# Second norm of three bridges from cross sums gathered in the layer ahead, residual update and scaling in one stream

## The reference

```python
def rms_norm(x, g):
    y = x * lax.rsqrt(jnp.mean(x * x, axis=-1, keepdims=True) + RMS_EPS)
    return y * g

x = x + gate * rms_norm(y, g1)                 # first norm and residual update
h = rms_norm(x, g2) * (1 + scale) + shift      # second norm, on the updated residual
out = squared_relu_mlp(h, w1, w2)              # or the next layer's projections
```

## Time and profile before

| | |
|---|---|
| median of 3 runs | 3150.22 us |
| profiled execution, time | 3138.47 us |
| profiled execution, span | 3136.6 us |
| mean granted TensorE clock | 0.953 of 2.4 GHz |
| TensorE matmul busy | 2850.1 us (91%) |
| VectorE busy | 1775.9 us (57%) |
| ScalarE busy | 1215.9 us (39%) |
| bridge A, first `grow` to the end of the first pair of products | 377.3 to 427.8 us |
| bridge B, the same | 1968.7 to 2004.0 us |
| bridge C, the same | 2349.6 to 2383.9 us |

### The profile page before, as it was taken

One profiled execution on the slowest core, in us unless ns is written; L12 is line 12 of the kernel. 1 busy time (PEld: TensorE's weight loads), 2 busy tenths in 40 slices (PEclk: granted clock), 3 DMA queues, 4 the chain that ended last, 5 costly groups with the idle time before them and its releaser, 6 DMA issues. The chain is left out here.

```text
span 3136.6 us, 66277 instructions
## 1 busy us (share of the span) xinstructions
PE 2850.1 (91%) x29060; PEld 2480.2 (79%) x29060; DVE 1775.9 (57%) x2747; ACT 1215.9 (39%) x1998; POOL 35.7 (1%) x57
## 2 busy tenths in 40 slices
PE   4988999999997997899989988899999898889998
PEld 4977989999996887677777776788877685778877
DVE  7655565645446644666666644655546644466632
ACT  4225343222224433555555543433324425354421
POOL 0011000000002000000000000000000000000000
PEclk9999889999996998999999998799998999999999
DMA  6320223343321323000000103255531210123322
GB/s 254 121 86 28 81 84 128 124 141 125 124 79 58 108 95 127 31 25 16 18 25 26 32 7 115 109 179 182 175 111 53 64 41 8 54 81 99 97 86 82
DMA packets 89980, 272.89 MB, mean 87 GB/s; under 512 B 9440, under 2 KB 14688, under 8 KB 89568
## 3 DMA queue, kind: packets, MB, share of 16 engines
q1 hardware_dynamic: 85088, 258.17, 24.3%
q10 hardware_dynamic: 4608, 10.49, 0.9%
HBM read 252.11 MB, written 16.52 MB: 86 GB/s over the span
## 5 line engine op out<-in xcount | busy, mean ns | idle before, releaser
L430 DVE TENSOR_TENSOR weights_low<-raw_weights,weights_high 128x1024 fp32r<-128x1024 f32 (+3 forms) x333 | 356.5, 1072 | 741.5 <-ACT weights_high L399 740.9
L399 ACT ACTIVATE weights_high<-raw_weights 128x1024 fp32r<-128x1024 f32 (+3 forms) x333 | 310.8, 935 | 993.7 <-PE psum L223 954.0
L223 PE MATMUL psum<-mlp_in_high,weights_high 128*128 128x512 f32 (+1 forms) x1120 | 371.2, 368 | 17.8 <-DVE mlp_in_low L861 12.8
L223 PE MATMUL psum<-mlp_in_low,weights_high 128*128 128x512 f32 (+1 forms) x1120 | 370.2, 367 | 0.0
L223 PE MATMUL psum<-mlp_in_high,weights_low 128*128 128x512 f32 (+1 forms) x1120 | 369.9, 367 | 0.0
L223 PEld LDWEIGHTS psum<-mlp_in_high,weights_high 128*128 128x128 f32 x1120 | 208.6, 190 | 45.0 <-issue 13.9
L223 PE MATMUL psum<-hidden_low,weights_high 128*128 128x384 f32 (+1 forms) x768 | 229.8, 353 | 0.0
L223 PE MATMUL psum<-hidden_high,weights_high 128*128 128x384 f32 (+1 forms) x768 | 229.7, 353 | 0.0
L223 PE MATMUL psum<-hidden_high,weights_low 128*128 128x384 f32 (+1 forms) x768 | 229.7, 353 | 0.0
L223 PEld LDWEIGHTS psum<-mlp_in_high,weights_low 128*128 128x128 f32 x1120 | 208.7, 190 | 24.3
L223 PEld LDWEIGHTS psum<-mlp_in_low,weights_high 128*128 128x128 f32 x1120 | 208.8, 190 | 24.0
(11 more groups left out here) (451 smaller groups left out, 5599.0 us busy)
## 6 DMA issues: line engine op xcount, KB each, us to landing
mod_space<-in_ada SPq DMA_DIRECT2D x112, 512.0 KB, 3.9
raw_weights<-in_mlp_w SPq DMA_DIRECT2D x96, 512.0 KB, 4.3
raw_weights<-in_w_up SPq DMA_DIRECT2D x44, 512.0 KB, 3.6
work<-in_ada SPq DMA_DIRECT2D x32, 512.0 KB, 5.1
raw_weights<-in_mlp_w SPq DMA_DIRECT2D x64, 256.0 KB, 3.0
raw_weights<-in_w_down SPq DMA_DIRECT2D x16, 512.0 KB, 3.5
raw_weights<-in_w_in SPq DMA_DIRECT2D x12, 512.0 KB, 4.8
raw_weights<-in_w_out SPq DMA_DIRECT2D x8, 512.0 KB, 3.9
```

The source lines that it names most:

```text
L223: last = nc.tensor.matmul(out[:, a, :] if wide else out, w[:, cols], x[:, at, t0:t1], start=first, stop=final)
L399: nc.scalar.activation(halves_of(ph, j)[0], raw_of(ph, j), ACT.Copy).then_inc(high.sem, 1)
L430: nc.vector.tensor_tensor(lo, raw_of(ph, j), hi.bitcast(F32), ALU.subtract).then_inc(split.sem, 1)
```

## The change

`CrossSums` takes the place of `FoldedSums` at the end of the three blocks ahead of the bridges. Beside the running total of y*y it keeps two more: of X*u and of u*u. Per tile ScalarE squares twice (the second time with the gain as its scale), and VectorE makes the product X*u and folds three totals (two of u*u and X*u and the old one). The gains `0x mix` and `0c mix` are derived one block earlier, and the buffers are reused (`pool_u` stays alive as the space of `Sides`).

`MergedBridge` takes the place of `Bridge`. TensorE sums the two cross totals (`cross`) behind the first spread; four small VectorE operations (`update`) correct the kept sum of squares of X; the second root comes from that. The residual need not be squared. The update of the later tiles and the scaling of the first ones run in one VectorE stream, five tiles apart. `grow` works in place in y, which also takes the scaled tile. Two earlier roots (opening of layer 0, token shift of layer 1) copy their sums of squares into `residual_squares` (one ScalarE copy each).

```diff
+class CrossSums:
...
+    def square(self, eng, k):
+        act = self.core.nc.scalar.activation
+        if k >= 2:
+            eng.wait_ge(self.folded.sem, self.step(k - 1, "y"))
+        act(self.sq if k else self.total, self.y(k), ACT.Square).then_inc(self.squared.sem, 1)
+        if k >= 2:
+            eng.wait_ge(self.folded.sem, self.step(k - 1, "gy"))
+        for t0, t1, c in self.gains:
+            last = act((self.gy if k else self.total_gy)[:, t0:t1], self.y(k)[:, t0:t1], ACT.Square, scale=col(c, k))
+        last.then_inc(self.squared.sem, 1)
+
+    def fold(self, dve, k):
+        nc = self.core.nc
+        dve.wait_ge(self.squared.sem, self.squared0 + 2 * k + 1)
+        if k >= 2:
+            dve.wait_ge(self.folded.sem, self.step(k - 1, "xy"))
+        for t0, t1, c in self.gains:
+            last = nc.vector.scalar_tensor_tensor((self.xy if k else self.total_xy)[:, t0:t1], self.y(k)[:, t0:t1], col(c, k),
+                                                  self.x(k)[:, t0:t1], ALU.mult, ALU.mult)
+        last.then_inc(self.folded.sem, 1)
+        if k == 0:
+            return
+        if k < self.kt - 1:
+            nc.vector.tensor_tensor(self.total, self.total, self.sq, ALU.add).then_inc(self.folded.sem, 1)
+        dve.wait_ge(self.folded.sem, self.step(k, "product"))
+        nc.vector.tensor_tensor(self.total_xy, self.total_xy, self.xy, ALU.add).then_inc(self.folded.sem, 1)
+        dve.wait_ge(self.squared.sem, self.squared0 + 2 * k + 2)
+        nc.vector.tensor_tensor(self.total_gy, self.total_gy, self.gy, ALU.add).then_inc(self.folded.sem, 1)
...
+    def cross(self, pe):
+        pe.wait_ge(self.folded.sem, self.step(self.kt - 1, "gy"))
+        for place, total in ((self.place_xy, self.total_xy), (self.place_gy, self.total_gy)):
+            for t in range(self.tokens // P):
+                last = self.core.nc.tensor.matmul(place[:, t:t + 1], total[:, t * P:(t + 1) * P], self.core.ones[:, 0:1],
+                                                  start=True, stop=True)
+        last.then_inc(self.crossed.sem, 1)
+
+    def update(self, dve, first):
+
+        nc, nt = self.core.nc, self.tokens // P
+        r, t, kept = first.small[:, 1, :], first.small[:, 3, :], self.core.residual_squares[:, 0:nt]
+        chain = Chain(dve, self.steps, self.steps0)
+        dve.wait_ge(self.crossed.sem, self.crossed0 + 1)
+        chain(nc.vector.tensor_tensor(t, self.place_gy, r, ALU.mult))
+        chain(nc.vector.scalar_tensor_tensor(t, self.place_xy, 2.0, t, ALU.mult, ALU.add))
+        chain(nc.vector.tensor_tensor(t, t, r, ALU.mult))
+        chain(nc.vector.tensor_tensor(kept, kept, t, ALU.add))
...
 class Root:
...
-        eng.wait_ge(*sums.complete())
-        nc.scalar.activation(self.small[:, 0, :], sums.place[:, 0:self.nt], ACT.Sqrt, bias=self.core.eps,
+        if self.updated is None:
+            eng.wait_ge(*sums.complete())
+        else:
+            eng.wait_ge(*self.updated)
+        src = sums.place[:, 0:self.nt] if self.updated is None else self.core.residual_squares[:, 0:self.nt]
+        if self.keep:
+            nc.scalar.activation(self.core.residual_squares[:, 0:self.keep], src[:, 0:self.keep], ACT.Copy)
+        nc.scalar.activation(self.small[:, 0, :], src, ACT.Sqrt, bias=self.core.eps,
...
+class MergedBridge(Bridge):
...
+    def scalar(self, eng, weights):
+        self.first.scalar(eng)
+        weights()
+        self.root.scalar(eng)
+        for k in range(self.kt):
+            self.scaling.shift(eng, k)
+
+    def tensor(self, pe):
+        self.first.tensor(pe)
+        self.sums.cross(pe)
+        self.root.tensor(pe)
+
+    def vector(self, dve, weights):
...
+        self.first.vector(dve)
+        dve.wait_ge(*self.first.ready())
+        grow(0)
+        grow(1)
+        add(0)
+        weights()
+        grow(2)
+        add(1)
+        self.sums.update(dve, self.first)
+        grow(3)
+        add(2)
+        self.root.vector(dve)
+        grow(4)
+        add(3)
+        dve.wait_ge(*self.root.ready())
+        for k in range(self.kt + 1):
+            n = k + self.AHEAD
+            if n < self.kt:
+                grow(n)
+            if k < self.kt:
+                scale(k)
+            if n <= self.kt:
+                add(n - 1)
+            if k >= 1:
+                self.scaling.low(dve, k - 1)
```

More of the change, by code:

```diff
@@ L797, in add, with __init__, step, complete @@
         ins.then_inc(self.summed.sem, 1)
+class CrossSums:
+    def __init__(self, core, y, x, gains, kt, tokens, space, totals):
+        self.core, self.y, self.x, self.gains, self.kt, self.tokens = core, y, x, gains, kt, tokens
+        self.total, self.sq, self.xy, self.gy = (space[:, i * tokens:(i + 1) * tokens] for i in range(4))
+        self.total_xy, self.total_gy = (totals[:, i * tokens:(i + 1) * tokens] for i in range(2))
+        nt = tokens // P
+        self.place = core.psum[:, 7, 256:256 + nt]
+        self.place_xy, self.place_gy = (core.psum[:, 5, 256 + 8 * i:256 + 8 * i + nt] for i in range(2))
+        names = ("cross_squared", "cross_folded", "cross_summed", "cross_done", "cross_step")
+        self.squared, self.folded, self.summed, self.crossed, self.steps = (counter(core, n) for n in names)
+        self.squared0, self.folded0, self.summed0, self.crossed0, self.steps0 = \
+            (counter(core, n).base for n in names)
+        self.squared.base += 2 * kt
+        self.folded.base += 1 + 4 * (kt - 2) + 3
+        self.summed.base += 2
+        self.crossed.base += 1
+        self.steps.base += 4
+    def step(self, k, which):
+        if k == 0:
+            return self.folded0 + 1
+        order = ("product", "y", "xy", "gy") if k < self.kt - 1 else ("product", "xy", "gy")
+        return self.folded0 + 1 + 4 * (k - 1) + order.index(which) + 1
+    def square(self, eng, k):
[17 more added lines that the diff above has]
+        last.then_inc(self.folded.sem, 1)
+        if k == 0:
+            return
[5 more added lines that the diff above has]
+        nc.vector.tensor_tensor(self.total_gy, self.total_gy, self.gy, ALU.add).then_inc(self.folded.sem, 1)
+    def complete(self):
+        return self.summed.sem, self.summed0 + 2
+    def add(self, pe, k):
+        if k < self.kt - 2:
+            return
+        last, nt = k == self.kt - 1, self.tokens // P
+        if last:
+            pe.wait_ge(self.squared.sem, self.squared0 + 2 * k + 1)
+        else:
+            pe.wait_ge(self.folded.sem, self.step(k, "y"))
+        for t in range(nt):
+            ins = self.core.nc.tensor.matmul(self.place[:, t:t + 1], (self.sq if last else self.total)[:, t * P:(t + 1) * P],
+                                             self.core.ones[:, 0:1], start=not last and t == 0, stop=last and t == nt - 1)
+        ins.then_inc(self.summed.sem, 1)
+    def cross(self, pe):
[14 more added lines that the diff above has]
+        chain(nc.vector.tensor_tensor(kept, kept, t, ALU.add))
+    def updated(self):
+        return self.steps.sem, self.steps0 + 4
@@ L957, in vector, with grow, add, scale @@
         self.scaling.low(dve, self.kt - 1)
+class MergedBridge(Bridge):
+    AHEAD = 5
+    def scalar(self, eng, weights):
[9 more added lines that the diff above has]
+    def vector(self, dve, weights):
+        nc = self.core.nc
+        def grow(k):
+            for t0, t1, c in self.gains:
+                last = nc.vector.scalar_tensor_tensor(self.y[:, k, t0:t1], self.y[:, k, t0:t1], col(c, k),
+                                                      self.first.rstd[:, t0:t1], ALU.mult, ALU.mult)
+            last.then_inc(self.grown.sem, 1)
+        def add(k):
+            dve.wait_ge(self.grown.sem, self.grown0 + k + 1)
+            nc.vector.tensor_tensor(self.X[:, k, 0:self.tokens], self.X[:, k, 0:self.tokens], self.y[:, k, 0:self.tokens], ALU.add)\
+                .then_inc(self.added.sem, 1)
+        def scale(k):
+            dve.wait_ge(self.added.sem, self.added0 + k + 1)
+            self.scaling.scale(dve, k)
+        self.first.vector(dve)
[23 more added lines that the diff above has]
+                self.scaling.low(dve, k - 1)
 class Opening(Bridge):
@@ L3022, in folded_sums, with cross_sums, merged_bridge @@
             return FoldedSums(core, src, DT, tokens, space, core.psum[:, bank, 256:256 + tokens // P])
+        def cross_sums(tokens, gains, space, totals):
+            return CrossSums(core, lambda k: Y[:, k, 0:tokens], lambda k: X[:, k, 0:tokens], gains, DT, tokens, space, totals)
+        def merged_bridge(tokens, scales, shifts, dst, space, cross, y, gains):
+            first = Root(core, cross, wide(tokens, 6))
+            root = Root(core, cross, wide(tokens, 4), updated=cross.updated())
+            scaling = Scaling(core, DT, tokens, lambda k: X[:, k, 0:tokens], root.rstd, scales, shifts, dst, space)
+            scaling.tmp = [y[:, k, 0:tokens] for k in range(DT)]
+            return MergedBridge(core, tokens, X, root, scaling, cross, y, gains, first)
```

(5 more changed lines are left out.)

42 lines of the change are left out of this document (25 added, 17 removed).

## The result

| | before | after |
|---|---|---|
| median of the runs | 3149.73 us (3144.36 to 3152.85, 4 runs) | 3114.31 us (3110.60 to 3120.51, 4 runs) |
| ratio | | 0.9891, 95% interval 0.9868 to 0.9914 |
| profiled execution | 3138.47 us | 3111.34 us (span 3109.2) |

A forecast was written before the change was run, and what follows sets the result against it. TensorE, 91% busy, was taken as the bound, with time to win in its bridge waits: 9.8 (A) + 6.8 (B) + 6.3 (C) - 0.2 = 22.7 us, from 3150.2 to 3127.5 us, range 3119.5 to 3138.5.

The forecast's parts named there:

- the bridges: Hand-overs A (after layer 0's `w_out`), B (after `rw_wo`), C (after layer 1's MLP): gains of 9.8, 6.8 and 6.3 us.
- The entries: Block ends ahead of the bridges: product and folds behind the last square delay A 1.65, B 1.0, C 1.15 us.
- The stream: VectorE from first `grow` to `low` of tile 0: 13.5 us in B (before 21.2), 18.7 in A.
- The small chain is hidden: In the bridges: cross sums end before `update`; second root and spreading lie under 2.5 us of `grow` and `add`.
- The cover in `w_out`: Block ahead of A: VectorE's added 2.95 us per step fit into 3.69 us idle, 0.7 to spare.
- The kept copy: Token shift's root: ScalarE copy of the kept sums on the path, 0.1 to 0.25 us, counted as 0.2 lost.
- rival 1: Product pairs: low clock lasts twice as long, 3134 us, chance 0.10; or through the pair, 3150, chance 0.03.
- the term for what the clock gives back: Pair in B: ends at 1997.1 if the clock returns after 5.7 us, 1996.1 if at once.
- Rivals 2, 3 and 4: 2: VectorE bounds `w_out`, 3155 us, 0.04; 3: bridge's end off the path, 3150, 0.05; 4: stream holes, 3132, within forecast.
- the median of the runs lies 11.75 above, and I carry the difference over: Whole kernel: median 11.75 us above the profiled 3138.47, so base 3150.2 less 22.7 gives 3127.5.
- medians here differ by some 2 us: Whole kernel: room for median spread, used with gains of 12 to 29 us to set the range.

The follow-up runs named there:

- in_turn: Changed kernel with its cross sums, but VectorE back in the old order; 3132.51 us, ratio 0.9964 to the kernel before.
- load: Changed kernel plus two useless VectorE products in every `w_out` step ahead of bridges A and B; 3131.37 us, one run.
- before_again: The kernel before, unchanged, measured against itself; 3142.26 us (12 runs), ratio 0.9992.
- after_third: The changed kernel, unchanged, measured a third time against the kernel before; 3118.21 us (4 runs), ratio 0.9909.
- after_again: The changed kernel, unchanged, measured a second time against the kernel before; 3118.39 us (6 runs), ratio 0.9909.
- lead: `early` (`update` one turn ahead), with the first weight split also put before the first `grow`; 3116.53 us (4 runs), ratio 0.9907 to the kernel before.
- early: Changed kernel with `update` and second root one turn ahead, stream four tiles ahead instead of five; 3114.28 us (4 runs), ratio 0.9907 to the kernel before.
- pool_adds: Changed kernel with each bridge's eight residual additions on GpSimd instead of VectorE; 3119.31 us (4 runs), ratio 0.9925 to the kernel before.
- warm: Changed kernel with useless large TensorE matmuls ahead of each bridge's first tile; 3118.81 us (4 runs), ratio 0.9916 to the kernel before.

## Why the prediction was right about the bridges and wrong about the time

- **The entries** (the first `grow`, counted from the last sums' start) came 1.6 and 0.96 us later in A and B, forecast 1.65 and 1.0. Right.
- **The stream**: 13.3 us in B, 18.4 in A, forecast 13.5 and 18.7. Right; `update` takes 0.79 and reads no later than planned. Tile 7 of B comes 24.7 us after the first `grow`; the prediction's own steps add up to 24.8, where it says 25.1. `in_turn` shows that the order, not the sums alone, carries the gain: it takes 15 us of it away.
- **The small chain is hidden**: right, though with a number wrong: the cross sums are two sets, so 24 and 16 matmuls (5.12 and 3.41 us), and I had counted 12 and 8. They end 2.3 us ahead of `update` in A and in B.
- **The cover in `w_out`**: 0.9 us of idle time left, forecast 0.7. Right, and `load` shows that it ends there.
- **The kept copy**, forecast 0.2 us: between the weight splits on both sides of the token shift lie 42.3 us in the first trace before and 43.1 after, but 43.1 also in `before_again` and 41.3 in `after_third`; too small to be told from how that stage differs by itself.
- **The pair's clock** (rival 1): the tiles came slowly, and the low clock did not last twice as long: in B 6.0 us, before 5.9, and 3.0 in both later traces; in A 4.5, before 3.5, which cost nothing. The rival fell. But the term for what the clock gives back was too small: I took the low stretch over as it was, and left out the second one behind the pair. Where both go well, B's pair ends 0.9 us earlier and the stage behind is 1.6 shorter: `after_again` against `before_again` gives 10.0 + 7.6 + 8.4 = 26.0 us for the three bridges, 2 more than the first pair of traces. That the change itself brings this about isn't shown.
- **Rivals 2, 3 and 4** did not come about: no VectorE-bound step, the bridge ends stayed on the path, no hole in the stream.

**The step that failed** is "the median of the runs lies 11.75 above, and I carry the difference over", with "medians here differ by some 2 us". The kernel before has had medians of 3149.7, 3144.5, 3142.6 and 3146.8 us in four comparisons, 7 us apart, and its profiled execution of 3138.47 was at the short end of what its runs gave, 3134 to 3157. I took a base from three runs as if it were the kernel's, and gave its spread 2 us of room in the range. (The range's terms are also summed wrong: they allow a gain of 22.7 + 2.1 + 2 = 26.8 at most, and 29 is stated.) From 3144.5, the base with the most runs, a gain of 22.7 would have been 3121.8, and one of 26.0 gives 3118.5, which is where the changed kernel's later medians lie (3118.39 and 3118.21). The first result, 3114.31, is 4 below these. So of the 13 us by which the forecast missed, some 6 are the base, 3 the bridges (2 the mis-sized clock term, 1 the rest), and 4 how four runs fell; the split is worked out from these medians and not tested by itself. In the first comparison itself the base came out at 3149.73, as taken, and the gain of 35.4 us is what is off there; its interval, 27 to 42, holds the 28.6 that `after_again` and `after_third` both give, so chance is the likelier reading and not a shown one. The later comparisons ran on three different chips, and whether the chip or the execution makes the medians differ stays open. Between 26.0 us by the traces and 28.6 by the ratios 2.6 us stay open, well inside the interval of 22 to 35.

## What to carry to other kernels

When a wait for a long chain of small operations is taken out of a hand-over, look at what the waiting engine does on either side of it: here putting 56 one-column sums in the place of 224 was worth 9.4 us, and the freedom to interleave that came with it 15. What then counts is the sum of that engine's work up to the last tile, so move work into its remaining waits (`lead`) before moving the first tile forward (`early`), and not to GpSimd, whose additions stretched VectorE's operations (`pool_adds`). And measure the base of a forecast: a median of three runs can be 5 us off in 3145, so a range must hold that before it holds any term of the sum.

## What the runs showed of the hardware that was not expected

- One program's untouched stage differs by 8 us between executions (896.6 and 904.8), and by 16 over kernels with the same code there, while the tiles of the bridges repeat to 0.02 us.
- The same pair of products in B gets the high clock back after 6.0 us in one execution and 3.0 in another, and a second low stretch of 3.4 us behind it comes or stays away, with the same 1.8 us of waiting between the pair and the next product in both. The tiles come at the same times in both (13.29 to 24.72 us after the first `grow`), so it isn't they that decide. Over the 13 traces the second stretch comes behind B's pair where the first lasted 5.7 to 6.2 us (six traces) and not where it lasted 5.1 or less (seven); the cause I could not show.
- The same nine matmuls of filling, 4.19 us long, ahead of a pair with the same tiles at the same times, brought the high clock in B and not in C (`warm`).
- A GpSimd addition of 512 columns takes 1.27 us and stretches a VectorE split from 1.17 to 2.0 us, and leaves an operation with one PSUM operand at 0.74.
